# Feed-forward pairs: five of seven products move 512 columns at once, and their halves are added behind

## What is computed

```python
def swiglu(x, w_in, w_out):
    gate, up = jnp.split(x @ w_in, 2, axis=-1)
    return (jax.nn.silu(gate) * up) @ w_out
...
    h = swiglu(rmsnorm(x, norm_ffn1_pre[l]), w_ffn1_in[l], w_ffn1_out[l])
    x = x + FFN_RESIDUAL_SCALE * rmsnorm(h, norm_ffn1_post[l])
```

## Time and profile before

| what | value |
|---|---|
| median of 3 runs | 1515.07 us |
| profiled execution | 1514.94 us |
| its span | 1513.3 us |
| granted TensorE clock | full speed in all 40 slices |
| nine pairs, first stage | 60.17 to 241.6 us |
| nine pairs, second stage | 635.18 to 816.6 us |

### The profile page before, as it was taken

How to read it: one execution, slowest core, us unless ns; L and a number is a source line. 1 busy time by engine, 2 the same in 40 slices (tenths; PEclk the granted TensorE clock), 3 DMA queues, 4 the chain that set the end, 5 groups by cost and what they waited for, 6 DMA issues and landing times.

```text
span 1513.3 us, 23600 instructions
## 1 busy us (share of the span) xinstructions
PE 1497.9 (99%) x9156; PEld 1343.9 (89%) x9156; DVE 1071.1 (71%) x1279; ACT 744.2 (49%) x1102; POOL 54.2 (4%) x101
## 2 busy tenths in 40 slices
PE   8999999999999999999999999999999999999998
PEld 7899998889988889899999888788888888889997
DVE  5888885326856847888886665788888865736873
ACT  6545443226566427544444234567676633344554
POOL 1000000001200002000000000100000000000001
PEclk9999999999999999999999999999999999999999
DMA  6233323232232222233335663222223132322331
GB/s 198 84 112 101 96 81 140 89 105 84 69 103 84 82 101 69 87 109 93 102 111 195 236 208 84 57 65 74 57 82 83 56 111 84 112 85 87 107 112 56
DMA packets 135044, 153.33 MB, mean 101 GB/s; under 512 B 3728, under 2 KB 123660, under 8 KB 134972
## 3 DMA queue, kind: packets, MB, share of 16 engines
q1 hardware_dynamic: 131712, 137.38, 28.9%
q0 software_dynamic: 3024, 14.88, 2.9%
q10 hardware_dynamic: 236, 0.06, 0.0%
HBM read 150.08 MB, written 2.23 MB: 101 GB/s over the span
## 4 chain that ended last, share of the span: by engine, by line
PE 96%; DVE 2%; ACT 1%; issue 0%; DMA 0%; DVEq 0%; ACTq 0%
PE ps L2532 20%; PE ps L2697 20%; PE ps L2534 19%; PE ps L2533 19%; PE ps L2702 10%; PE ps L2897 1%; PE ps L3003 1%; PE ps L3013 1%; PE ps L2983 1%; PE ps L2982 1%; PE ps L3012 1%; PE ps L2615 0%; PE ps L2964 0%; PE ps L2675 0%; DVE wl L1544 0%
## 5 line engine op out<-in xcount | busy, mean ns | idle before, releaser
L2532 PE MATMUL ps<-ah,wh 128*128 128x512 f32 (+1 forms) x1136 | 431.7, 380 | 3.8 <-DVE wl L1945 1.4
L2534 PE MATMUL ps<-ah,wl 128*128 128x512 f32 (+1 forms) x1136 | 425.6, 375 | 0.0
L2533 PE MATMUL ps<-al,wh 128*128 128x512 f32 (+1 forms) x1136 | 425.2, 374 | 0.0
L1544 DVE TENSOR_TENSOR wl<-raw,wh 128x2048 fp32r<-128x2048 f32 x59 | 135.2, 2291 | 191.2 <-ACT wh L831 191.0
L2532 PEld LDWEIGHTS ps<-ah,wh 128*128 128x128 f32 x1136 | 213.9, 188 | 43.3 <-issue 2.3
L2534 PEld LDWEIGHTS ps<-ah,wl 128*128 128x128 f32 x1136 | 213.8, 188 | 38.9
L2533 PEld LDWEIGHTS ps<-al,wh 128*128 128x128 f32 x1136 | 214.1, 188 | 35.5
L831 ACT ACTIVATE wh<-raw 128x2048 fp32r<-128x2048 f32 x60 | 114.7, 1911 | 236.7 <-PE ps L2534 233.0
L2697 PE MATMUL ps<-al,wh 128*128 128x256 f32 x704 | 172.7, 283 | 0.0
L2697 PE MATMUL ps<-ah,wh 128*128 128x256 f32 x704 | 172.7, 283 | 0.0
L2697 PEld LDWEIGHTS ps<-al,wh 128*128 128x128 f32 x704 | 135.2, 192 | 0.1
(11 more groups left out here) (436 smaller groups left out, 2535.6 us busy)
## 6 DMA issues: line engine op xcount, KB each, us to landing
raw<-in_w_ffn_in SPq DMA_DIRECT2D x74, 512.0 KB, 3.6
raw<-in_w_in SPq DMA_DIRECT2D x52, 512.0 KB, 4.4
raw<-in_w_ffn_out SPq DMA_DIRECT2D x22, 1024.0 KB, 5.0
ada_raw<-in_w_ada POOLq DMA_DIRECT2D x8, 1536.0 KB, 7.2
raw<-in_w_mix_in SPq DMA_DIRECT2D x10, 1024.0 KB, 5.4
raw<-in_w_ffn_in SPq DMA_DIRECT2D x7, 1024.0 KB, 5.3
raw<-in_w_in SPq DMA_DIRECT2D x6, 1024.0 KB, 5.6
raw<-in_w_mix_out SPq DMA_DIRECT2D x4, 1024.0 KB, 5.0
```

Of the source, the lines that this page charges most:

```text
L1544: nc.vector.tensor_tensor(wl[n % 2][:], raw[n % 2][:], wh[n % 2][:].bitcast(fp32), ALU.subtract).then_inc(lo_done, 2 if n + 1 in AHEAD else 1)
L2532: nc.tensor.matmul(bank, w[0], m[0], start=start, stop=False, skip_group_check=shared)
L2533: nc.tensor.matmul(bank, w[0], m[1], start=False, stop=False, skip_group_check=shared)
L2534: return nc.tensor.matmul(bank, w[1], m[0], start=False, stop=stop, skip_group_check=shared)
```

## The change

**TensorE.** The high and the low activations now lie in one tile (`both`, `both_sums`), 256 columns of one and 256 of the other as one moving operand of 512. In the first two feed-forward stages B11, T2, T3, T4 and B21 go through `sided`: 8 matmuls of 512 columns with `wh` take the place of 16 of 256, and the 8 with `wl` stay. The result of a column block is now a whole bank: its left half holds wh·a_high + wl·a_high, its right half wh·a_low, and the two halves have still to be added. B11, T2, T3, T4 use banks 0 and 1 or 6 and 7 by the parity of the pair, B21 banks 2 and 3. T1 and B22 stay as they were, in bank 5. T1 now waits until the pair before has read bank 5 (`joined`), T4 for the first of three joins instead of the second, since the second gate is now read first.

**The halves.** ScalarE copies both halves (`sided_product`: two copies for `up1` and two for `gate1`; `last_side` one more for the last product). POOL gets a list of its own (`sides`): in each pair it adds the copied right half to `up1` and to `gate1`, and it makes the two multiplications by the norm's factor that VectorE had. VectorE adds both halves from PSUM in turn for `gate2` (`sided_join`) and `up1` (`up_join`), and for the last product adds in `whole2` and then multiplies. Between two such steps it waits for itself. ScalarE's silu of the first gate moves behind `high(1)`.

```diff
@@ -113,6 +113,7 @@
+SIDE = 6
...
-        ah = sb("ah", [P, KD, T], f32r)
-        al = sb("al", [P, KD, T], f32r)
+        both = sb("both", [P, 2, KD, T], f32r)
+        ah, al = both[:, 0], both[:, 1]
...
-            sh = sb("sh", [P, 3, KD // 2, T // 2], f32r, where=phase)
-            sl = sb("sl", [P, 3, KD // 2, T // 2], f32r, where=phase)
+            both_sums = sb("both_sums", [P, 2, 3, KD // 2, T // 2], f32r, where=phase)
+            sh, sl = both_sums[:, 0], both_sums[:, 1]
+            whole2 = sb("whole2", [P, 2, T // 2], where=phase)
...
+        up1_side, gate1_side = (tile[:].rearrange("p (c t) -> p c t", c=2) for tile in (acc, h7))
...
+        def high_side(par):
+
+            return ps[:, SIDE * par:SIDE * par + 2, 0:T // 2]
+
+        def low_side(par):
+
+            return ps[:, SIDE * par:SIDE * par + 2, T // 2:T]
+
+        def both_of(f, name):
+
+            if name == "T3":
+                return both_sums[:, :, 1, :, :]
+            low, high = slice(0, KD // 2), slice(KD // 2, KD)
+            return both[:, :, high if name in ("B21", "T4") else low, COLS[name in ("T2", "T4")]]
@@ -759,6 +778,39 @@
+            def sides(f):
+
+                r_half = [rstd[:, COLS[h]].unsqueeze(1).to_broadcast([P, 2, T // 2]) for h in range(2)]
+                first = SEVEN_AT[f]
+
+                def added(i, n, step, tile, side):
+
+                    pool.wait_ge(copied, i * 6 + (3 * n + step))
+                    nc.gpsimd.tensor_tensor(tile[:], tile[:], side, ALU.add).then_inc(side_added, 1)
+
+                def scaled(i, n, h, tile):
+
+                    pool.wait_ge(joined, i * 6 + (3 * n + 2 - h))
+                    nc.gpsimd.tensor_tensor(tile[:], tile[:], r_half[h], ALU.mult).then_inc(gate_ready, 1)
+
+                def pair(i, par):
+
+                    n = first + par
+                    added(i, n, 1, up1, up1_side)
+                    added(i, n, 3, gate1, gate1_side)
+                    scaled(i, n, 1, gate2)
+                    scaled(i, n, 0, gate1)
+
+                pool.wait_ge(gt_done, PLAIN_AT[f] + PLAIN[f])
+                pair(0, 0)
+                pair(0, 1)
+                with pool.Fori(1, SEVEN[f] // 2) as i:
+                    pair(i, 0)
+                    pair(i, 1)
+                if SEVEN[f] % 2:
+                    pair(SEVEN[f] // 2, 0)
+
+            sides(0)
             pool.wait_ge(rlo_done, 2)
             nc.gpsimd.memset(gh[:].bitcast(fp32), 0.0)
...
+            sides(1)
@@ -1007,6 +1060,11 @@
+                def last_side(i, par):
+
+                    act.wait_ge(hid_ready, i * 2 + (f * NFO + PLAIN[f] + par))
+                    nc.scalar.activation(whole2[:], low_side(par % 2), ACT.Copy).then_inc(side_copied, 1)
+
                 def pair(i, par, begin=False, end=False):
 
                     n = first_pair + par
@@ -1015,10 +1073,14 @@
                         act.wait_ge(p_used, i * 2 * PRODS + (PRODS * n + k))
 
                     def product(target, bank):
-                        nc.scalar.activation(target[:], ps[:, bank, :].rearrange("p (c t) -> p c t", c=2), ACT.Copy).then_inc(copied, 1)
+                        nc.scalar.activation(target[:], by_pair(ps[:, bank, :]), ACT.Copy).then_inc(copied, 1)
+
+                    def sided_product(target, side):
+                        nc.scalar.activation(target[:], high_side(par % 2), ACT.Copy)
+                        nc.scalar.activation(side, low_side(par % 2), ACT.Copy).then_inc(copied, 1)
 
                     def gate(h):
-                        act.wait_ge(gate_ready, i * 4 + (2 * n + h + 1))
+                        act.wait_ge(gate_ready, i * 4 + (2 * n + 2 - h))
...
+                        last_side(i, par - 1)
...
-                    product(up1, BANK1[par % 2])
+                    sided_product(up1, up1_side)
                     high(4, i, n)
                     used(2)
                     product(gate2, BANK5)
                     high(5, i, n)
                     used(3)
-                    product(gate1, BANK1[par % 2])
...
-                    gate(0)
...
+                    gate(0)
...
+                last_side((SEVEN[f] - 1) // 2, (SEVEN[f] - 1) % 2)
@@ -1797,14 +1860,17 @@
                     if h == 0:
-                        dve.wait_ge(gate_silu, i * 4 + (2 * n + 1))
+                        dve.wait_ge(gate_silu, i * 4 + (2 * n + 2))
                         dve.wait_ge(joined, i * 6 + (3 * n + 3))
                         nc.vector.tensor_tensor(at, at, up1[:], ALU.mult).then_inc(half_done, 1)
                     else:
-                        dve.wait_ge(gate_silu, i * 4 + (2 * n + 2))
+                        dve.wait_ge(gate_silu, i * 4 + (2 * n + 1))
                         dve.wait_ge(p_used, i * 2 * PRODS + PRODS * (n + 1))
                         dve.wait_ge(half_done, i * 2 + (n + 1))
-                        nc.vector.tensor_tensor(at, ps[:, BANK1[par % 2], :].rearrange("p (c t) -> p c t", c=2), at, ALU.mult).then_inc(hid_ready, 1)
+                        dve.wait_ge(side_copied, i * 2 + (n + 1))
+                        nc.vector.tensor_tensor(whole2[:], high_side(par % 2), whole2[:], ALU.add).then_inc(last_joined, 1)
+                        dve.wait_ge(last_joined, i * 2 + (n + 1))
+                        nc.vector.tensor_tensor(at, whole2[:], at, ALU.mult).then_inc(hid_ready, 1)
 
@@ -1822,11 +1888,17 @@
-                        nc.vector.tensor_tensor(tile[:], ps[:, bank, :].rearrange("p (c t) -> p c t", c=2), tile[:], ALU.add).then_inc(joined, 1)
-
-                    def scaled(tile, h):
-                        dve.wait_ge(joined, i * 6 + (3 * n + h + 1))
-                        nc.vector.tensor_tensor(tile[:], tile[:], r_half[h], ALU.mult).then_inc(gate_ready, 1)
+                        nc.vector.tensor_tensor(tile[:], by_pair(ps[:, bank, :]), tile[:], ALU.add).then_inc(joined, 1)
+
+                    def up_join():
+                        nc.vector.tensor_tensor(up1[:], ps[:, 2:4, 0:T // 2], up1[:], ALU.add).then_inc(up_joined, 1)
+                        dve.wait_ge(up_joined, i * 2 + (n + 1))
+                        nc.vector.tensor_tensor(up1[:], ps[:, 2:4, T // 2:T], up1[:], ALU.add).then_inc(joined, 1)
+
+                    def sided_join(tile):
+                        nc.vector.tensor_tensor(tile[:], high_side(par % 2), tile[:], ALU.add).then_inc(high_joined, 1)
+                        dve.wait_ge(high_joined, i * 2 + (n + 1))
+                        nc.vector.tensor_tensor(tile[:], low_side(par % 2), tile[:], ALU.add).then_inc(joined, 1)
 
                     if begin:
                         plain_hidden(PLAIN[f] - 1)
...
+                    sided_join(gate2)
                     dve.wait_ge(copied, i * 6 + (3 * n + 3))
+                    dve.wait_ge(side_added, i * 4 + (2 * n + 2))
                     join(gate1, BANK5)
                     if not end:
                         weight_sum("T2", i, n + 1)
-                    scaled(gate1, 0)
                     if end:
                         unit(1)
-                    used(5)
-                    join(gate2, BANK1[par % 2])
                     if not end:
                         low(0, i, n + 1)
-                    scaled(gate2, 1)
                     if end:
                         out_half(0)
                     used(6)
-                    join(up1, BANK2)
+                    up_join()
                     if not end:
                         low(1, i, n + 1)
                         weight_sum("T3", i, n + 1)
@@ -2676,6 +2747,21 @@
                 if part == 5:
                     last.then_inc(ada_mm, 1)
 
+            def sided(f, i, n, k, par):
+
+                name = PRODUCTS[k]
+                moving, base = both_of(f, name), 2 if name == "B21" else SIDE * par
+                for nb in range(2):
+                    for kk in range(KD // 2):
+                        nc.tensor.matmul(ps[:, base + nb, :].rearrange("p (s t) -> p s t", s=2), ring_of(wh, f, k)[:, kk, nb * P:(nb + 1) * P],
+                                         moving[:, :, kk, :], start=name in OPENS and kk == 0, stop=False, skip_group_check=True)
+                pe.wait_ge(p_lo, i * 2 * PRODS + (PRODS * n + k + 1))
+                for nb in range(2):
+                    for kk in range(KD // 2):
+                        last = nc.tensor.matmul(ps[:, base + nb, 0:T // 2], ring_of(wl, f, k)[:, kk, nb * P:(nb + 1) * P], moving[:, 0, kk, :],
+                                                start=False, stop=kk == KD // 2 - 1, skip_group_check=True)
+                last.then_inc(p_used, 1)
+
             def products(f, i, par, begin=False):
 
                 n = SEVEN_AT[f] + par
@@ -2686,10 +2772,17 @@
                     if name in ("T2", "B22", "T3"):
                         pe.wait_ge(copied, i * 6 + (3 * n + ("T2", "B22", "T3").index(name) + 1))
                     elif name == "T4":
```

(24 more changed lines are left out.)

6 lines of the change are left out of this document (4 added, 2 removed).

## The result

The changed kernel takes 1543.93 us (median of 4 runs, 1543.56 to 1544.83) against 1514.99 us (1514.86 to 1515.26) for the one before on the same chip: a ratio of 1.0192, 95% interval 1.0174 to 1.0209. It is slower by 28.9 us, where 16.4 were forecast and the range ended at 26. The profiled execution took 1543.56 us, its span is 1541.9 us.

A forecast was written before the change was run, and what follows sets the result against it. TensorE (busy 99%) bounds the kernel before; with POOL's turns VectorE needs 20.9 us a changed pair. Slower pairs and end holes, less the first two pairs' gain, add 8.2 us a stage, 16.4 in all: 1531.5 us, range 1508 to 1541.

The forecast's parts named there:

- a hole: At each stage's end, TensorE waits for the second `out_half` ahead of the first output slot: 3.9 us.
- The first rival, no turns: POOL and VectorE do not exclude each other, or overlap little; pairs take 19.63 us, 1508 us in all; chance 0.17.
- its condition: The no-turns outcome decides from the point where POOL costs VectorE under 1.84 us a pair instead of 3.1.
- the sizes of the turns: VectorE's delay from POOL where both read SBUF, up to 1.05 us per POOL instruction: 3.1 us a pair.
- the two full ones: POOL's scaling of `gate1` against T2 sum and `low(0)`, its addition to `gate1` among low parts: 1.05 us each.
- the two in which I let a neighbour hide part of the turn: POOL's scaling of `gate2`, 0.55 us on the T2 sum, and its addition to `up1`, 0.45 us.
- 17.79: VectorE's own list in a changed pair, us: 17.33 of instructions plus 0.46 of waits for itself, without POOL's effect.
- The first two pairs: At each stage's start VectorE still has slack, so they take 19.7 and 19.8 us, 0.8 less than before.
- The clock: TensorE's clock stays at full speed, as gaps up to some us left it before; no time added.
- The full-turn rival: Each POOL instruction costs VectorE 1.27 us instead of 1.05; a pair 21.7 us, 1545 us in all; chance 0.08.
- TensorE's gain: One 512-column matmul for two of 256 spares 0.0133 us; 720 of them give 9.6 us.
- What was costed at nothing: ScalarE's further copies, POOL's own length, weight DMAs, new waits of T1, B21 and T4, the later silu: no time.

The follow-up runs named there:

- experiment 1: The changed kernel with POOL's four instructions on 4 columns instead of 512, same waits and order: 1510.28 us.
- experiment 2: The changed kernel with POOL's four instructions on 256 columns instead of 512: 1511.78 us.
- experiment 4: The changed kernel with all work, but POOL's addition to `gate1` waits for `low(6)` and its scaling of `gate1` for the next `low(0)`: 1516.78 us.
- experiment 5: The kernel before, plus only four unused POOL additions a pair on the change's triggers: 1533.82 us.
- experiment 9: experiment 4 with VectorE making the last pair's scalings itself, and that pair's list reordered: 1507.68 us.
- experiment 12: experiment 5 with two of the four POOL additions let go later, by the second join of the gates and the join of `up1`: 1519.01 us.
- experiment 6: The changed kernel with all four POOL instructions of a pair moved to VectorE: 1540.48 us.
- experiment 11: experiment 6 with the two additions of copied halves moved behind `low(4)` and `low(6)`: 1529.67 us.

## Why the prediction was wrong in size and right in kind

**Right: who, where and why.** POOL's four instructions stretch VectorE's, the same four that the prediction named, VectorE becomes the bound, TensorE waits before T2, and the end has a hole: 4.00 us for a forecast 3.9. Experiments 1, 2 and 4 show that nothing else makes the pairs longer, and experiment 5 that POOL is enough. The first rival, no turns, falls with the rows of 2.3 us. That its price, 1508, is so near experiment 9 (1507.68) is chance: it had 9.6 us of gain and two holes of 1.2, experiment 9 has 7.4 and no hole. What experiments 4 and 9 do bear out is its condition, that TensorE is the bound again once POOL costs VectorE less than 1.84 us a pair: the two turns that are left cost some 1.4.

**The step that failed: the sizes of the turns.** The sum was 0.55 + 1.05 + 0.45 + 1.05 = 3.1. Measured: T2 sum 0.72, `low(0)` 1.10, hidden half 0.54 and 0.11 more before it, `low(5)` 1.09, in all 3.56. The two full ones were near; the two in which I let a neighbour hide part of the turn were each 0.2 too small. In both, POOL started later behind that neighbour than I had put: 0.16 us behind the join of `gate1` (118.34 to 118.50) instead of 0.10, and 0.20 behind the addition in `whole2` (128.49 to 128.69) instead of 0.12; the rest is the full turn of 1.1 for 1.05. With 17.79, which was right, 3.56 gives 21.35, against 21.36 measured, and not 20.9. As VectorE is the bound, each tenth counts in 14 pairs: 14 x 0.46 = 6.4 us.

**The first two pairs.** I gave them 19.7 and 19.8 us, from VectorE's slack. It had next to none: in the first pair its timeline shows two stretched sums.

```profile
64.83 2.32 DVE L1851 TENSOR_TENSOR t<-raw,sq 128x1024 f32<-128x1024 f32 x1
...
70.48 2.31 DVE L1851 TENSOR_TENSOR tt<-raw 128x1024 f32<-128x1024 f32 x1
```

189.7 - 7 x 21.36 leaves 20.1 for each of the two, and 189.4 in the second stage 19.9: 0.7 and 0.4 us more than I said, 1.1 in all. TensorE waits before T2 in eight pairs of nine, not seven.

**The clock, the second step that failed.** I wrote that it stays at full speed, as gaps up to some us had left it before. But the longest gap of TensorE behind other matmuls in the kernel before is 1.4 us, and I forecast holes of 3.9. Behind each the clock fell, which cost 4.0 us in all; the sum has no term for it. Without this, or without the sizes of the turns, the time would have stayed inside the range. The full-turn rival at 1545 comes nearest to the time, but not by its mechanism; it asked for 1.27 us a turn and 21.7 a pair.

6.4 + 1.1 + 4.0 = 11.5 of the 12.4 us between 1531.5 and 1543.93; the two holes add 0.2, and 0.7 stays open.

**TensorE's gain** was taken as 9.6 us and is 7.4 in experiment 9. Eight matmuls of 512 columns in `sided` take 1.84 us, 0.230 each instead of 0.227; that is 2.2 us of 720 matmuls. I had taken this loss at nothing; it gave no time in the changed kernel, where VectorE is the bound. Whether the moving operand in two pieces causes it was not tried.

**What was costed at nothing** held: TensorE's waits in the two stages name no weight DMA, and none stands ahead of T4 or T1. ScalarE's copy ends the gap before T2, as forecast, but at VectorE's pace: it had itself waited 2.37 us for the hidden half.

The Trainium skill (SBUF — State Buffer, Who interferes with whom) says that a VectorE instruction with at most one SBUF input, outside its 2-port modes, does not contend with GpSimd. By that rule, the trace of experiment 4 agrees: POOL takes 1.30 us beside PSUM additions of 0.68 and 0.69, as each does alone.

## What to carry to other kernels

An engine that makes the bound's instructions longer is no free place for work; but when it works can count for more than how much it does. The same four GpSimd instructions cost 33.6 us with one set of waits and 6.5 with another (experiments 1 and 4), in the old kernel 18.7 and 3.9 (5 and 12): let them start where VectorE reads PSUM or waits anyway. Moving them back to VectorE gained 3.4 us in one order and 14.3 in another (experiments 6 and 11). Idle time in a row is slack only if what ends it would not move with the work in front of it (experiment 5), and a list that fits does not mean a round that fits: add up the way from engine to engine and back (experiment 6). Price a hole of TensorE at its length and the slow matmuls behind it, and move the next stage's first operands ahead to close it.
